# Grouped and differential attention of a layer as one stage over one list of items

## The chip, the cores and the metric

The kernel runs on one core of one Trainium2 chip. The core has a matrix engine (TensorE, PE in the rows; PEld is its weight load), a vector engine (VectorE, DVE), an activation engine (ScalarE, ACT), GpSimd (POOL) and SyncE (SP), which issues the DMAs. The time is the device time of one execution in microseconds. The median of three runs before the change is 3674.05 us (3666.71 to 3675.09).

## What is computed

The program is two models one behind the other on 512 tokens of width 1024, in float32. The second has two layers, and each layer holds two attentions over the same tokens. Everything else (projections, a state-space scan, a gated merge, a mixture of experts) is as it was. The two attentions of one layer, cut to what matters:

```python
def gqa_block_attention(q, k, v):          # 4 query heads of 64, 2 key heads
    scale = d ** -0.5
    ...
        logits = jnp.einsum('bqgrd,bkgd->bgrqk', qi, k).astype(jnp.float32) * scale
        probs = jax.nn.softmax(logits, axis=-1).astype(v.dtype)
        return jnp.einsum('bgrqk,bkgd->bqgrd', probs, v)
...
def diff_block_attention(q1, q2, k1, k2, v, lam, rel_bias):   # 4 heads, queries of 32
    ...
        p1 = jax.nn.softmax(jnp.einsum('bqhd,bkhd->bhqk', q1i, k1).astype(jnp.float32) * scale + bias, axis=-1)
        p2 = jax.nn.softmax(jnp.einsum('bqhd,bkhd->bhqk', q2i, k2).astype(jnp.float32) * scale + bias, axis=-1)
        w = (p1 - lam * p2).astype(v.dtype)
        return jnp.einsum('bhqk,bkhd->bqhd', w, v)
...
    for i in range(DEPTH):
        ...
        o_a = gqa_block_attention(q, k, a_v.reshape(b, s, A_KV_HEADS, A_HEAD_DIM))
        ...
        o_c = (rms_norm(o_c, g_diff[i]) * (1.0 - lam_init)).reshape(b, s, DIFF_HEADS * DIFF_V_DIM)
        ...
        branches = jnp.stack([o_a, o_b, o_c, o_d], axis=2)
```

## The kernel before

The program is a chain of stages. A stage (`stage`, L231) is one block of instruction streams, one stream for each engine, with its own semaphores. At its end all engines meet (L239 in the rows is the branch behind that meeting), so no instruction of the next stage starts before the slowest engine is through. Inside a stage each engine runs its stream in the written order and waits on semaphores. In each layer the stages are the projections (`mix_project`), the scan (`ssm_scan`), `grouped`, `differential`, `merge`, `out_stage`, then the mixture of experts.

`grouped` and `differential` both build a list of items and hand it to the same three routines, one for each engine. An item is two score maps of 128 queries against 512 keys, held in two PSUM banks (banks 0 and 1 for even items, 2 and 3 for odd ones). The steps of an item n, by the names that the texts use:

- **score(n)**, TensorE, L1027: two products, one for each map. Grouped items have 64 rows, differential ones 32.
- **shift(n)**, VectorE: the negative row maximum. A grouped item takes one reduction over both maps (L1096) and a tiny product (L1097), and its scores stay in PSUM. A differential item takes two custom instructions with their read-outs (L1102), which add the bias table and write the sums to SBUF.
- **exps(n)**, ScalarE: two exponentials with row sums (L1072 grouped, reading PSUM; L1075 differential, in SBUF in place).
- **weigh(n)**, VectorE: the reciprocal (L1110) and the division, two instructions for a grouped item (L2034), three for a differential one (L2184 to L2186), whose two maps become one.
- **turn(n)**, TensorE, L1036: transposes into banks 6 and 7, eight for a grouped item (two maps), four for a differential one.
- **copy(n)**, ScalarE, L1083: the transposed maps from PSUM to SBUF, 1024 or 512 columns.
- **values(n)**, TensorE, L1044: products with the values, sixteen matrix instructions for a grouped item, eight for a differential one, into bank 4 (first half of the items) or bank 5 (second half).

TensorE's stream is score(0), score(1), and then for each n: score(n+2), turn(n), values(n-1), and values of the last item at the end. ScalarE's is exps(0), and for each n exps(n+1), copy(n). VectorE's is shift(0), and for each n shift(n+1), weigh(n). There are three score buffers in SBUF (`SB`) and two for the transposed maps (`PT`).

`grouped` has 8 items. Banks 4 and 5 hold its result; when the values of all 8 are summed, ScalarE copies both banks to SBUF (L2056) and the stage ends. At its start SyncE issues the load of the bias table (L2044, 1792 KB), into memory that the scan used until then, and waits for it. `differential` has 16 items, again into banks 4 and 5, and a norm over each head: ScalarE squares and copies a bank (L2218, L2219) behind item 9 and at the end, TensorE sums and spreads (L2200, L2210), VectorE multiplies (L2239).

## Time and profile before

| | us |
|---|---|
| median of three runs (lowest, highest) | 3674.05 (3666.71, 3675.09) |
| profiled execution, its device time | 3673.06 |
| its span, first to last instruction | 3671.3 |
| TensorE busy | 3474.4 (95% of the span) |
| VectorE busy | 1718.2 (47%) |
| ScalarE busy | 1147.7 (31%) |
| mean granted TensorE clock | 0.969 of full speed |

TensorE's busy time is no measure of its pace, because its instructions overlap and their ends are modelled; a start time is read instead. PEclk is the clock that TensorE was granted, as a share of 2.4 GHz: 1.00 is 2.4 GHz, 0.50 is 1.2 GHz, and a value between is a stretch with both. In a timeline row the bracket tells how long the engine was idle before the row and what released it.

### The profile page before, as it was taken

Reading aid. Unit: us, or ns where it says so; the run is one execution under the profiler, and the core shown is the slowest. Engines: PE = TensorE matmul, PEld = TensorE weight load, DVE = VectorE, ACT = ScalarE, POOL = GpSimd, SP = SyncE. Lnnn points to the kernel's source line nnn. Section 1 sums busy time; section 2 is a strip of 40 time slices with the busy share of each in tenths; the row PEclk is TensorE's granted clock in tenths of the full one; section 3 lists DMA queues with packets and bytes.
Section 4 is the critical chain, followed back from the end, with each engine's and each line's share of the span. In section 5 each row is a group of like instructions: output and inputs, shape, how many; then the busy total and the mean of one; then the engine's idle time right before and its main releaser. Section 6 shows DMA issues by size and latency. Waiting matters only on the chain. (4 is left out here: it accounts for less than half of the span.)

```text
span 3671.3 us, 44737 instructions
## 1 busy us (share of the span) xinstructions
PE 3474.4 (95%) x16808; PEld 2376.3 (65%) x16808; DVE 1718.2 (47%) x2898; ACT 1147.7 (31%) x1816; POOL 41.5 (1%) x20
## 2 busy tenths in 40 slices
PE   8899999989999999989998999999988997999997
PEld 6678877855788886746875444437756886444436
DVE  6665545468665537566334111137656334111116
ACT  6632223147422224365322000013355333000003
POOL 0000000022000000000000000000000000000000
PEclk9999999999999999989999999999988998999998
DMA  4223322210133231211225999991211324999992
GB/s 153 89 91 94 96 91 97 81 71 1 69 97 96 92 97 55 70 61 55 98 95 203 405 421 422 422 381 58 90 61 34 98 80 173 376 421 422 422 421 82
DMA packets 113080, 618.90 MB, mean 169 GB/s; under 512 B 12780, under 2 KB 13300, under 8 KB 63544
## 3 DMA queue, kind: packets, MB, share of 16 engines
q1 hardware_dynamic: 112952, 617.18, 44.1%
q8 instruction: 82, 1.34, 0.1%
q14 instruction: 46, 0.38, 0.0%
HBM read 614.95 MB, written 4.28 MB: 169 GB/s over the span
## 5 line engine op out<-in xcount | busy, mean ns | idle before, releaser
L400 PE MATMUL PS<-WK_r,RING_r 128*128 128x512 f32 x1920 | 748.7, 390 | 0.0
L398 PE MATMUL PS<-WK_r 128*128 128x512 f32 x1448 | 565.1, 390 | 0.8 <-DVE RING_r L395 0.8
L400 PEld LDWEIGHTS PS<-WK_r,RING_r 128*128 128x128 f32 x1920 | 360.0, 187 | 77.2
L392 ACT ACTIVATE WK_r<-RING 128x1024 fp32r<-128x1024 f32 x212 | 223.4, 1054 | 449.7 <-PE PS L400 369.9
L399 PE MATMUL PS<-HT_r,WK_r 128*128 128x512 f32 (+1 forms) x896 | 348.6, 389 | 0.0
L395 DVE TENSOR_TENSOR RING_r<-RING,WK_r 128x1024 fp32r<-128x1024 f32 x212 | 259.0, 1221 | 184.9 <-ACT WK_r L392 184.8
L398 PEld LDWEIGHTS PS<-WK_r 128*128 128x128 f32 x1448 | 271.3, 187 | 58.4 <-DVE RING_r L395 1.3
L399 PE MATMUL PS<-HT_r,RING_r 128*128 128x512 f32 (+1 forms) x752 | 296.4, 394 | 0.0
L400 PE MATMUL PS<-AR_r,RING_r 128*128 128x512 f32 x672 | 262.9, 391 | 0.0
L395 DVE TENSOR_TENSOR RING_r<-RING,RING_r 128x1280 fp32r<-128x1280 f32 (+2 forms) x96 | 132.3, 1380 | 275.3 <-ACT RING_r L392 275.3
L398 PE MATMUL PS<-AR_r,RING_r 128*128 128x512 f32 x640 | 251.2, 392 | 9.1 <-DVE HT_r L395 9.1
L399 PE MATMUL PS<-AR_r,WK_r 128*128 128x512 f32 (+1 forms) x552 | 214.7, 389 | 0.0
L392 ACT ACTIVATE RING_r<-RING 128x1280 fp32r<-128x1280 f32 (+2 forms) x96 | 113.6, 1185 | 288.3 <-PE PS L400 263.2
L2644 DVE TENSOR_TENSOR XT<-XT,PS 128x512 f32<-128x512 f32 x128 | 82.1, 684 | 235.9 <-PE PS L2540 235.9
L399 PEld LDWEIGHTS PS<-HT_r,WK_r 128*128 128x128 f32 (+1 forms) x896 | 167.7, 187 | 35.8 <-issue 0.5
L2524 PE MATMUL PS<-AR,WK 128*64 128x512 f32 x768 | 171.6, 595 | 0.0
L395 DVE TENSOR_TENSOR AR_r<-AR,WK_r 128x512 fp32r<-128x512 f32 (+1 forms) x74 | 51.2, 692 | 239.8 <-ACT WK_r L392 239.6
L399 PEld LDWEIGHTS PS<-HT_r,RING_r 128*128 128x128 f32 (+1 forms) x752 | 141.8, 189 | 32.3 <-issue 1.3
L2658 DVE TENSOR_TENSOR HT<-HT,PS 128x512 f32<-128x512 f32 x32 | 20.6, 684 | 301.6 <-PE PS L2510 301.6
L2491 PEld LDWEIGHTS PS<-WK 128*128 128x128 f32 x896 | 107.4, 191 | 68.2 <-issue 68.2
L400 PEld LDWEIGHTS PS<-AR_r,RING_r 128*128 128x128 f32 x672 | 127.3, 189 | 26.5
L398 PEld LDWEIGHTS PS<-AR_r,RING_r 128*128 128x128 f32 x640 | 121.2, 189 | 35.3 <-DVE RING_r L395 9.9
(458 smaller groups left out, 5357.5 us busy)
## 6 DMA issues: line engine op xcount, KB each, us to landing
AR<-moe SPq DMA_DIRECT2D x192, 1024.0 KB, 16.4
RING<-moe SPq DMA_DIRECT2D x160, 1024.0 KB, 15.9
RING<-ff_in SPq DMA_DIRECT2D x96, 512.0 KB, 3.5
RING<-branch SPq DMA_DIRECT2D x64, 640.0 KB, 3.8
WK<-moe SPq DMA_DIRECT2D x32, 1024.0 KB, 17.7
RING<-ff_out SPq DMA_DIRECT2D x48, 512.0 KB, 3.5
RING<-mix_in SPq DMA_DIRECT2D x44, 512.0 KB, 3.5
RING<-ple SPq DMA_DIRECT2D x16, 640.0 KB, 9.1
```

The costliest lines, as they stand in the source:

```text
L392: return nc.scalar.activation(r(out), x, ACT.Copy)
L395: return nc.vector.tensor_tensor(r(out), x, r(high).bitcast(F32), ALU.subtract)
L398: nc.tensor.matmul(out, r(w_high), r(x_high), start=start, stop=False)
L399: nc.tensor.matmul(out, r(w_high), r(x_low), start=False, stop=False)
L400: return nc.tensor.matmul(out, r(w_low), r(x_high), start=False, stop=stop)
L2491: mm = nc.tensor.matmul(bank(k // 4, (k % 4) * P, P), HN[:, t, k * P:(k + 1) * P], HOTS[parity][:, t], start=(t == 0), stop=(t == TT - 1))
L2524: mm = nc.tensor.matmul(bank(4 + half)[e * CAP:(e + 1) * CAP], HI[:, k, e * CAP:(e + 1) * CAP], w[:, (2 * row + e) * TOK:(2 * row + e + 1) ...
L2644: v.tensor_tensor(XT[:, k], XT[:, k], bank(k - 4 if spread else 6 + k % 2), ALU.add).then_inc(s["added"], 1)
L2658: v.tensor_tensor(HID[:, half], SG[:, half], bank(2 + half), ALU.mult).then_inc(s["hidden"], 1)
```

## The change

`grouped` and `differential` become one stage, `attention`, with one list of 24 items: the 8 grouped ones (0 to 7) and behind them the 16 differential ones (8 to 23, `FIRST` is 8). The three routines take a list of both kinds: how many signals an item of either kind gives is counted from the list (`shifted`, and the sum over `values`), where it was a fixed multiple. The grouped results leave their banks while later items run: ScalarE copies bank 4 behind copy(5) and bank 5 behind copy(9) (`output`), and TensorE waits for that copy before the first values of item 8 (bank 4) and of item 16 (bank 5) (`bank_free`). The load of the bias table keeps its place at the stage's start, and VectorE waits for it before shift(8).

```diff
@@ -1014,24 +1014,26 @@
             self.scores, self.bias, self.weigh, self.values, self.outs = scores, bias, weigh, values, outs
             self.scale = scale
 
-    def att_pe(pe, s, items, then=lambda n: None):
-        maps = len(items[0].values)
-
+    def shifted(items, n):
+
+        return sum(1 if x.bias is None else 2 for x in items[0:n + 1])
+
+    def att_pe(pe, s, items, then=lambda n: None, before=lambda n: None):
         def score(n):
             if n >= 2:
-                if items[n].bias is None:
+                if items[n - 2].bias is None:
                     pe.wait_ge(s["exped"], 2 * (n - 1))
                 else:
-                    pe.wait_ge(s["maxed"], 2 * (n - 1))
+                    pe.wait_ge(s["maxed"], shifted(items, n - 2))
             for m, (q, k) in enumerate(items[n].scores):
                 mm = nc.tensor.matmul(bank(2 * (n % 2) + m), q, k, start=True, stop=True)
             mm.then_inc(s["scored"], 1)
 
         def turn(n):
-            pe.wait_ge(s["weighed"], maps * (n + 1))
+            pe.wait_ge(s["weighed"], sum(len(x.values) for x in items[0:n + 1]))
             if n:
                 pe.wait_ge(s["copied"], n)
-            for m in range(maps):
+            for m in range(len(items[n].values)):
                 for kb in range(TT):
                     mm = nc.tensor.transpose(bank(6 + m, kb * P, P), SB[n % 3][:, m, kb * P:(kb + 1) * P], cst("ident"))
             mm.then_inc(s["turned"], 1)
@@ -1039,6 +1041,7 @@
         def values(n):
             x = items[n]
             pe.wait_ge(s["copied"], n + 1)
+            before(n)
             for kb in range(TT):
                 for m, out in enumerate(x.outs):
                     mm = nc.tensor.matmul(out, x.values[m][kb], PT[n % 2][:, m, kb * P:kb * P + P],
@@ -1057,15 +1060,13 @@
         values(len(items) - 1)
 
     def att_act(act, s, items, then=lambda n: None):
-        maps = len(items[0].values)
-
         def exps(n):
             if items[n].bias is None:
-                act.wait_ge(s["maxed"], n + 1)
+                act.wait_ge(s["maxed"], shifted(items, n))
                 if n >= 3:
                     act.wait_ge(s["turned"], n - 2)
             else:
-                act.wait_ge(s["maxed"], 2 * (n + 1))
+                act.wait_ge(s["maxed"], shifted(items, n))
             for m in range(2):
                 buf = SB[n % 3][:, m]
                 if items[n].bias is None:
@@ -1080,6 +1081,7 @@
             act.wait_ge(s["turned"], n + 1)
             if n >= 2:
                 act.wait_ge(s["summed_v"], n - 1)
+            maps = len(items[n].values)
             nc.scalar.activation(PT[n % 2][:, 0:maps], PS[:, 6:6 + maps], ACT.Copy).then_inc(s["copied"], 1)
 
         exps(0)
@@ -1098,6 +1100,8 @@
                 return
             if n >= 3:
                 dve.wait_ge(s["turned"], n - 2)
+            if items[n - 1].bias is None:
+                dve.wait_ge(s["bias"], 16)
             for m in range(2):
                 nc.vector.tensor_tensor_reduce(SB[n % 3][:, m], bank(2 * (n % 2) + m), items[n].bias, 1.0, 3e38,
                                                ALU.add, ALU.min, NM[n % 3][:, m:m + 1]).then_inc(s["maxed"], 1)
@@ -2025,40 +2029,16 @@
                     evict(f"ck{c}", ar(CK + c))
 
 
-    def grouped(l):
-        with stage("bias o_out" + ATT) as (block, s):
-            items = []
-            for c in range(2):
-                for t in range(TT):
-                    def weigh(step, p, rc, co):
-                        return [nc.vector.tensor_scalar(p[:, m], p[:, m], rc[:, m:m + 1], None, ALU.mult)
-                                for m in range(2)]
-
-                    halves = [slice(0, 64), slice(64, 128)]
-                    items.append(Item([(ar(AQ + c)[rows, t * P:(t + 1) * P], ar(AK)[rows]) for rows in halves], None, weigh,
-                                      [[VM[:, kb, q * 64:q * 64 + 64] for kb in range(TT)] for q in range(2)],
-                                      [bank(4 + c, t * P, P)[rows] for rows in halves], RQ[:, t, 2 * c:2 * c + 2]))
-
-            @block.sync
-            def _(sp):
-                sp.dma_start(BIAS, skewed).then_inc(s["bias"], 16)
-                sp.wait_ge(s["bias"], 16)
-
-            @block.tensor
-            def _(pe):
-                att_pe(pe, s, items)
-
-            @block.scalar
-            def _(act):
-                att_act(act, s, items)
-                act.wait_ge(s["summed_v"], len(items))
-                for c in range(2):
-                    nc.scalar.activation(wk(BR + c), bank(4 + c), ACT.Copy).then_inc(s["o_out"], 1)
-
-            @block.vector
-            def _(dve):
-                step = Steps(dve, s["dve_step"])
-                att_dve(dve, s, step, items)
+    def grouped_items():
+
+        def weigh(step, p, rc, co):
+            return [nc.vector.tensor_scalar(p[:, m], p[:, m], rc[:, m:m + 1], None, ALU.mult) for m in range(2)]
+
+        halves = [slice(0, 64), slice(64, 128)]
+        return [Item([(ar(AQ + c)[rows, t * P:(t + 1) * P], ar(AK)[rows]) for rows in halves], None, weigh,
+                     [[VM[:, kb, q * 64:q * 64 + 64] for kb in range(TT)] for q in range(2)],
+                     [bank(4 + c, t * P, P)[rows] for rows in halves], RQ[:, t, 2 * c:2 * c + 2])
+                for c in range(2) for t in range(TT)]
 
 
     def ssm_scan(l):
@@ -2169,11 +2149,18 @@
 
 
     BIAS = ar(7, 7).rearrange("p (h m) -> p h m", h=4)
-    def differential(l):
+    def attention(l):
         RH = SM[:, 312:312 + 4 * TT].rearrange("p (t c h) -> p t c h", t=TT, c=2)
         lam_init = 0.8 - 0.6 * float(np.exp(-0.3 * l))
-        with stage("o_done" + ATT + HEAD_NORM) as (block, s):
-            items = []
+        with stage("bias o_out o_done" + ATT + HEAD_NORM) as (block, s):
+            items = grouped_items()
+            FIRST = len(items)
+
+            @block.sync
+            def _(sp):
+                sp.dma_start(BIAS, skewed).then_inc(s["bias"], 16)
+                sp.wait_ge(s["bias"], 16)
+
             for c in range(2):
                 for hh in range(2):
                     h = 2 * c + hh
@@ -2201,7 +2188,11 @@
                                               start=True, stop=True)
                     mm.then_inc(s["hn_summed"], 1)
 
-                att_pe(pe, s, items, lambda n: head_sums(0) if n == 10 else None)
+                def bank_free(n):
+                    if n in (FIRST, FIRST + 8):
+                        pe.wait_ge(s["o_out"], 1 + (n - FIRST) // 8)
+
+                att_pe(pe, s, items, lambda n: head_sums(0) if n == FIRST + 10 else None, bank_free)
                 head_sums(1)
                 pe.wait_ge(s["hn_inverse"], 1)
                 for c in range(2):
@@ -2214,11 +2205,21 @@
             @block.scalar
             def _(act):
                 def square(c):
-                    act.wait_ge(s["summed_v"], 8 * (c + 1))
+                    act.wait_ge(s["summed_v"], FIRST + 8 * (c + 1))
                     nc.scalar.activation(wk(10 + c), bank(4 + c), ACT.Square).then_inc(s["hn_squared"], 1)
                     nc.scalar.activation(wk(BR + 4 + c), bank(4 + c), ACT.Copy, scale=par("diff_g", l)).then_inc(s["hn_copied"], 1)
 
-                att_act(act, s, items, lambda n: square(0) if n == 9 else None)
+                def output(c):
+                    act.wait_ge(s["summed_v"], TT * (c + 1))
+                    nc.scalar.activation(wk(BR + c), bank(4 + c), ACT.Copy).then_inc(s["o_out"], 1)
+
+                def between(n):
+                    if n in (TT + 1, 2 * TT + 1):
+                        output(n // TT - 1)
+                    if n == FIRST + 9:
+                        square(0)
+
+                att_act(act, s, items, between)
                 square(1)
                 act.wait_ge(s["hn_mean"], 1)
                 nc.scalar.activation(RH, RH, ACT.Sqrt).then_inc(s["hn_root"], 1)
@@ -2758,8 +2759,7 @@
     for l in range(LAYERS):
         mix_project(l)
         ssm_scan(l)
-        grouped(l)
-        differential(l)
+        attention(l)
         merge(l)
         out_stage(mix_out[l], arc, load_router(l), None if l else (lambda k: nc.vector.scalar_tensor_tensor(
             out=XT[:, k], in0=XT[:, k], scalar=par("final1_g", k), in1=R1, op0=ALU.mult, op1=ALU.mult)))
```

ScalarE, around the end of the grouped items in layer 0. Before (L1072 and L1075 are the exponentials, L1083 the copies of transposed maps, L2056 the copies of the grouped result):

```order
L1072 ACTIVATE WK,SM<-PS,SM 128x512 x2
L1083 ACTIVATE WK<-PS 128x1024
L1072 ACTIVATE WK,SM<-PS,SM 128x512 x2
L1083 ACTIVATE WK<-PS 128x1024 x2
L2056 ACTIVATE WK<-PS 128x512 x2
L239 UNCONDITIONAL_BRANCH
L2214 UNCONDITIONAL_BRANCH
L1075 ACTIVATE WK,SM<-WK,SM 128x512 x4
L1083 ACTIVATE WK<-PS 128x512
```

After, with L1073 and L1076 for the exponentials, L1085 for the copies of maps and L2214 for the copy of one result bank:

```order
L1085 ACTIVATE WK<-PS 128x1024
L2214 ACTIVATE WK<-PS 128x512
L1073 ACTIVATE WK,SM<-PS,SM 128x512 x2
L1085 ACTIVATE WK<-PS 128x1024
L1076 ACTIVATE WK,SM<-WK,SM 128x512 x2
L1085 ACTIVATE WK<-PS 128x1024
L1076 ACTIVATE WK,SM<-WK,SM 128x512 x2
L1085 ACTIVATE WK<-PS 128x512
L1076 ACTIVATE WK,SM<-WK,SM 128x512 x2
L1085 ACTIVATE WK<-PS 128x512
L2214 ACTIVATE WK<-PS 128x512
```

The two result copies stood together in front of the branch; now each stands alone between a copy of maps and the next exponentials, four items apart.

TensorE, the same place in layer 0. Before (L1036 transposes, L1044 values, L1027 scores), from the transposes of item 6:

```order
L1036 MATMUL PS<-CST,WK 128x128 x8
L1044 MATMUL PS<-WK,AR 64x128 x8
L1036 MATMUL PS<-CST,WK 128x128 x8
L1044 MATMUL PS<-WK,AR 64x128 x16
L239 UNCONDITIONAL_BRANCH
L2195 UNCONDITIONAL_BRANCH
L1027 MATMUL PS<-AR 128x512 x6
L1036 MATMUL PS<-CST,WK 128x128 x4
L1027 MATMUL PS<-AR 128x512 x2
L1036 MATMUL PS<-CST,WK 128x128 x4
L1044 MATMUL PS<-WK,AR 64x128 x4
```

After, with L1029 for the scores, L1038 for the transposes and L1047 for the values, from the scores of item 8:

```order
L1029 MATMUL PS<-AR 128x512 x2
L1038 MATMUL PS<-CST,WK 128x128 x8
L1047 MATMUL PS<-WK,AR 64x128 x8
L1029 MATMUL PS<-AR 128x512 x2
L1038 MATMUL PS<-CST,WK 128x128 x8
L1047 MATMUL PS<-WK,AR 64x128 x8
L1029 MATMUL PS<-AR 128x512 x2
L1038 MATMUL PS<-CST,WK 128x128 x4
L1047 MATMUL PS<-WK,AR 64x128 x8
L1029 MATMUL PS<-AR 128x512 x2
L1038 MATMUL PS<-CST,WK 128x128 x4
L1047 MATMUL PS<-WK,AR 64x128 x4
```

The branch is gone, and the scores of items 8 and 9 stand in front of the transposes of items 6 and 7. VectorE, the same place, before (L1110 reciprocal, L2034 division, L1102 bias and maximum):

```order
L1096 TENSOR_REDUCE SM<-PS 128x2
L1097 TENSOR_TENSOR SM<-SM 128x2
L1110 RECIPROCAL SM<-SM 128x2
L2034 TENSOR_SCALAR WK<-WK,SM 128x512 x2
L1110 RECIPROCAL SM<-SM 128x2
L2034 TENSOR_SCALAR WK<-WK,SM 128x512 x2
L239 UNCONDITIONAL_BRANCH
L2226 UNCONDITIONAL_BRANCH
L1102 ISA WK,SM<-PS,AR 128x512
L1102 ISA SM 128x1
```

After (L1114 reciprocal, L2035 division, L1106 bias and maximum), from the division of item 6:

```order
L2035 TENSOR_SCALAR WK<-WK,SM 128x512 x2
L1106 ISA WK,SM<-PS,AR 128x512
L1106 ISA SM 128x1
L1106 ISA WK,SM<-PS,AR 128x512
L1106 ISA SM 128x1
L1114 RECIPROCAL SM<-SM 128x2
L2035 TENSOR_SCALAR WK<-WK,SM 128x512 x2
L1106 ISA WK,SM<-PS,AR 128x512
L1106 ISA SM 128x1
L1106 ISA WK,SM<-PS,AR 128x512
L1106 ISA SM 128x1
L1114 RECIPROCAL SM<-SM 128x2
```

The shifts of items 8 and 9 now stand in front of the weighing of items 7 and 8.

## Rows read from the trace of the kernel before

**Rows 1.** Busy time by stretch: both attention stages together, layer 0 and layer 1

```profile
core 0: us, PE busy (x) PEld busy (x) DVE busy (x) ACT busy (x) POOL busy (x), PEclk, DMA share, GB/s
...
1598.04:1691.24 93.20, 81.90 (x528) 49.66 (x528) 64.73 (x172) 59.39 (x129) 0.00 (x0) 0.87 0.06 21
...
2716.70:2811.93 95.23, 84.50 (x528) 51.36 (x528) 64.91 (x172) 59.36 (x129) 0.00 (x0) 0.84 0.06 21
```

**Rows 2.** Timeline, grouped items in layer 0, at their steady pace

```profile
1618.76 1.09 PE L1036 MATMUL PS<-CST,WK 128*128 128x128 f32 x8
...
1619.89 1.02 ACT L1083 ACTIVATE WK<-PS 128x1024 f32<-128x1024 f32 x1 [0.56 <-PE PS L1036]
...
1620.81 1.13 PE L1027 MATMUL PS<-AR 64*128 64x512 f32 x4
...
1621.87 1.09 PE L1036 MATMUL PS<-CST,WK 128*128 128x128 f32 x8
```

**Rows 3.** Timeline, from the last grouped item to the first differential one, layer 0

```profile
1627.75 2.28 PE L1044 MATMUL PS<-WK,AR 128*64 128x128 f32 x32
...
1630.07 1.08 ACT L2056 ACTIVATE WK<-PS 128x512 f32<-128x512 f32 x2 [1.20 <-PE PS L1044]
...
1631.46 1.99 PE L1027 MATMUL PS<-AR 32*128 32x512 f32 x8 [1.44 <-PEq L239]
...
1637.26 1.12 PE L1036 MATMUL PS<-CST,WK 128*128 128x128 f32 x4 [1.19 <-DVE WK L2186]
```

**Rows 4.** Timeline, TensorE's transposes and VectorE of differential items 3 to 12, layer 0

```profile
1644.69 0.69 DVE L1102 CUSTOM_DVE_ANT_0 WK<-PS,AR 128x512 f32<-128x512 f32 x1 [1.36 <-PE PS L1027]
...
1647.63 0.66 PE L1036 MATMUL PS<-CST,WK 128*128 128x128 f32 x4 [0.33 <-DVE WK L2186]
...
1650.43 0.66 PE L1036 MATMUL PS<-CST,WK 128*128 128x128 f32 x4
...
1670.52 0.66 PE L1036 MATMUL PS<-CST,WK 128*128 128x128 f32 x4 [0.19 <-DVE WK L2186]
...
1674.17 0.66 PE L1036 MATMUL PS<-CST,WK 128*128 128x128 f32 x4
```

**Rows 5.** Timeline, transposes around the same seam in layer 1

```profile
2739.57 1.09 PE L1036 MATMUL PS<-CST,WK 128*128 128x128 f32 x8
...
2755.43 1.12 PE L1036 MATMUL PS<-CST,WK 128*128 128x128 f32 x4 [1.21 <-DVE WK L2186]
...
2758.48 1.11 PE L1036 MATMUL PS<-CST,WK 128*128 128x128 f32 x4
...
2763.43 1.12 PE L1036 MATMUL PS<-CST,WK 128*128 128x128 f32 x4
...
2770.68 0.66 PE L1036 MATMUL PS<-CST,WK 128*128 128x128 f32 x4 [0.33 <-DVE WK L2186]
```

**Rows 6.** Busy time by stretch (columns as Rows 1), around the seam, layers 0 and 1

```profile
1622.00:1631.00 9.00, 7.29 (x88) 5.85 (x88) 3.38 (x8) 5.95 (x11) 0.00 (x0) 1.00 0.00 0
...
1634.00:1640.00 6.00, 4.81 (x12) 1.72 (x12) 5.42 (x16) 4.49 (x12) 0.00 (x0) 0.50 0.00 0
...
1646.00:1655.00 9.00, 8.41 (x53) 4.73 (x50) 8.58 (x27) 6.61 (x16) 0.00 (x0) 1.00 0.00 0
...
2760.00:2765.00 5.00, 5.00 (x18) 2.84 (x18) 2.82 (x9) 2.05 (x6) 0.00 (x0) 0.50 0.01 3
```

**Rows 7.** Issue and landing of the bias table in layer 0

```profile
AR<-bias_spread SPq DMA_DIRECT2D x1, 1792.0 KB, 7.6
```

**Rows 8.** Timeline of SyncE: first DMAs behind the attention, both layers

```profile
1691.24 0.81 SPq L259 DMA_DIRECT2D RING<-mix_out  x2
...
1965.61 2.48 SPq L2365 DMA_DIRECT2D RING<-moe  x5
...
2811.93 0.81 SPq L259 DMA_DIRECT2D RING<-mix_out  x2
...
3086.29 2.45 SPq L2365 DMA_DIRECT2D RING<-moe  x5
```

## Prediction

> **What bounds the kernel now.** The first view is the busy time by stretch. The two attention stages together take 93.20 us in layer 0 and 95.23 us in layer 1 [rows 1], 188.4 us of a span of 3671.3 us, so the change can touch one twentieth of the program. The reader should see there that no engine fills this stretch (TensorE 81.90, VectorE 64.73, ScalarE 59.39 of 93.20 us) and that the same instructions take 2.03 us longer in layer 1 at a lower clock (0.84 against 0.87).
>
> The second view is the timeline, to see who waits at the steady pace. A grouped item takes 3.11 us (transposes at 1618.76 and 1621.87) and TensorE shows no idle time ahead of its rows, while ScalarE waits 0.56 us in each item [rows 2]. TensorE bounds the grouped items. A differential item takes 2.86 us: from 1647.63 to 1670.52 there are eight of them [rows 4], and there TensorE waits 0.33 and 0.19 us for VectorE. VectorE bounds these: from the start of its shift at 1644.69 to the transposes that follow its weighing at 1647.63 are 2.94 us [rows 4].
>
> The third view is the seam between the stages. TensorE's last grouped values begin at 1627.75, ScalarE then copies the result for 1.08 us, all engines meet, the first differential scores start at 1631.46 after 1.44 us of idle time, and the first differential transposes come at 1637.26 [rows 3]. The clock was 1.00 until 1631, is 0.50 from 1634 to 1640 and 1.00 again from 1646 on; in layer 1 it is still 0.50 at 2760 to 2765 [rows 6]. So the seam costs three things: a pipeline that runs empty and fills again, the meeting itself, and a stretch at 1.2 GHz instead of 2.4 GHz.
>
> **The change, part by part.** I price it as one interval, from the transposes of grouped item 5 to those of differential item 4, which is item 12 of the merged list. Ahead of it nothing in TensorE's stream changes, behind it both kernels are at the steady pace.
>
> Before, layer 0: 1650.43 - 1621.87 = 28.56 us [rows 2, 4]. Before, layer 1: 2770.68 - 2739.57 = 31.11 us [rows 5].
>
> After, the interval holds seven items' steps. The scores of item 8 go where scores always stand, one item's pace behind those of item 7: 1620.81 + 3.10 = 1623.91 [rows 2]. The waits of item 8 have been met by then: the exponentials of item 6 that free its banks run ahead of those scores, and the bias table, issued at the start of the stage, lands after 7.6 us [rows 7] and is needed only some 27 us in. The three steps of TensorE's loop follow each other at 1.06, 1.02 and 1.02 us (scores at 1620.81 to transposes at 1621.87 is the first [rows 2]; the other two share the rest of 3.11), so the transposes of items 6, 7 and 8 come at 1624.97, 1628.07 and 1631.17, still bound by TensorE. VectorE keeps up: the scores of item 9 start at 1627.01 and take 1.13 us [rows 2], so its shift starts at about 1628.25 and item 8 is weighed 2.94 us later, at 1631.19. The scores of item 10 start at 1630.11 and end at 1631.24; its shift starts at 1631.35, and the transposes of item 9 follow at 1634.29. From here VectorE is the bound at 2.86 us: item 12 at 1634.29 + 3 x 2.86 = 1642.87. That makes 21.0 us for the interval. For layer 1 I take the same 21.0 us, since the clock is as high there ahead of the seam.
>
> - Layer 0: 28.56 - 21.0 = 7.6 us gone. Layer 1: 31.11 - 21.0 = 10.1 us gone. Together 17.7 us.
>
> The added work is ScalarE's result copies, two in each layer. They are not new, they only move, 0.54 us each [rows 3]. Behind copy(5) the copy of bank 4 falls into the 0.56 us in which ScalarE waits in each grouped item [rows 2]. In numbers: copy(4) ends at 1619.89 + 1.02 = 1620.91, copy(5) one pace later at 1624.02, the result copy at 1624.56, and the two exponentials of item 7, which fill what is left of an item (3.11 - 0.56 - 1.02 = 1.53 us), at 1626.09. VectorE wants them only behind the shift of item 8, whose two instructions of 0.69 us [rows 4] start at 1625.15 and are through at 1626.5. Behind copy(9) ScalarE has more room still. So I take nothing for them. If that cover is gone, the nearest row is the place where the kernel already squares and copies a bank inside the list, behind differential item 9: the transposes stand 3.65 us apart there (1670.52 to 1674.17 [rows 4]), 0.8 us over the pace, with sums of the head norm on TensorE in it as well. That bounds an insertion at 0.8 us, 3.2 us for four. From below, no item can be faster than 2.86 us; if all seven were, the interval would be 20.0 us, a further 2.0 us for both layers.
>
> The two waits of TensorE for the freed banks (ahead of the first values of items 8 and 16) have the values queued behind them, and VectorE waits for nobody there; the copies they wait for end about 10 us (bank 4) and 20 us (bank 5) earlier. VectorE's wait for the bias table has the shift of item 8 behind it and is long met. These cost nothing.
>
> What lies behind the attention moves as a whole. SyncE issues nothing of it inside the attention; the first load of the experts comes 274.37 us after the merge's first load in layer 0 and 274.36 us in layer 1 [rows 8]. So neither transfers nor clock behind the attention depend on how long it took, and the gain is not given back there.
>
> The sum against the profiled execution's own time: 3673.06 - 17.7 = 3655.4 us. The profiled execution lies 1.0 us under the median of the three runs, 3674.05, which is inside their spread of 8.4 us. With the bounds of the copies and of the pace this case reaches from 3653.4 to 3658.6 us.
>
> **The rivals.**
>
> Rival 1: the clock falls near the old seam all the same. For it speaks that it falls at 1634, where TensorE has been idle for no more than 1.44 us at a time [rows 3, 6]. Against it: in the merged list TensorE has the scores of items 8 and 9 to do where it now waits. Its price is the part of the present gain that the clock makes: from the first to the fifth differential transposes are 13.17 us in layer 0 (1637.26 to 1650.43 [rows 3, 4]) and 15.25 us in layer 1 [rows 5] where four items at the pace take 11.44 us; 1.7 + 3.8 = 5.5 us. That gives 3655.4 + 5.5 = 3660.9 us.
>
> Rival 2, the slower one: the clock stays low for much of the merged list. The differential items leave TensorE a small gap in each item [rows 4], and two TensorE groups of different kinds now alternate. An item fully at 1.2 GHz takes 4.95 us (2758.48 to 2763.43 [rows 5]), 2.09 us over the pace. The gain is used up from 17.7 / 2.09 = 8.5 such items in the two lists of 16; if half of them, 16, ran so, the loss would be 33.4 us and the time 3655.4 + 33.4 = 3688.8 us. Against it: with the same gaps the clock is 1.00 from 1646 on [rows 6]. The Trainium skill says in "TensorE: Matmul & The Clock Gate", section "A second HAM failure mode: psum-queue depth-cycling", that a kernel which cycles through PSUM banks and idles briefly between groups of matmuls lets its clock swing between the two levels and loses throughput to it; by that rule this would be the outcome. By that rule, the trace disagrees so far.
>
> Rival 3: the lists interlock badly where they meet. Scores wait on another signal for a differential item than for a grouped one, and if one of the engines meets an empty queue once, a whole item's latency shows. The price is that of a first item's chain, 5.80 us from first scores to first transposes (1631.46 to 1637.26 [rows 3]) less the 2.86 us it would have taken: 2.9 us in each layer, 3661.3 us. The step by step reckoning above speaks against it; it rests on start times of before.
>
> Rival 4: the gain is hidden or given back, because the experts' loads or another later stage set the end whatever comes first; 3673 us. The rows of SyncE speak against it [rows 8].
>
> **How the numbers follow.** The forecast has 0.70, rival 1 has 0.13, rival 2 has 0.03, rival 3 has 0.09, rival 4 has 0.05. The predicted time is 3655.4 us. For the range, the low end is the forecast's own, 3653.4, less half the spread of the runs, 4.2: 3649 us. The high end takes in rivals 1 and 3 with some of that spread: 3664 us. A measurement of this kernel can tell about 0.3%, 11 us, from no change, so faster means under 3663.0 us. The forecast lies there nearly whole (0.67), rivals 1 and 3 lie just under the bound (0.12 of their 0.22). That makes faster 0.79, same 0.18 with rival 4 and the rest, slower 0.03.
>
> **What would show it.** In the changed profile the attention of layer 0 should take 85.6 us and of layer 1 85.1 us, nearly alike, with a mean clock above 0.9 in both. The transposes of items 5 and 12 should stand 21.0 us apart in both. The clock should be 0.50 only at the stage's start and not again before the head norm. Between the transposes of items 8 and 9 there should be about 3.1 us, afterwards 2.86 us. ScalarE's two result copies should have TensorE and VectorE unmoved behind them. The merge's first load should come 7.6 us earlier than now, and the last instruction 17.7 us earlier. I am wrong if the clock is 0.50 in the middle of the list, if an item around the meeting of the two kinds takes over 4 us, or if the stretches behind the attention have grown.

## The result, and the profile after

The changed kernel took 3653.20 us, the median of 5 runs (3647.95 to 3656.47), beside 3666.71 us for the kernel before in the same comparison, also 5 runs. The ratio is 0.9949 (0.9936 to 0.9962). Two more comparisons of the same pair, on two different chips, gave 0.9955 (0.9942 to 0.9969) and 0.9960 (0.9947 to 0.9974). Over all comparisons the median is 3670.52 us for the kernel before (75 runs, 3661.51 to 3681.38) and 3654.58 us for the changed one (15 runs, 3647.95 to 3658.81). The ratios are not the quotients of two medians (of the first comparison that would be 0.9963), so the gain is best given as a span: 15.9 us by the medians over all comparisons, 18.7, 16.5 and 14.7 us (of 3670) by the three ratios, 13.5 us by the medians of the first comparison. That is 0.4 to 0.5%. I had forecast 17.7 us and 3655.4 us.

The busy time by stretch of the changed kernel, for the attention of both layers, and for the merged list of each layer without its first items and its head norm. Columns as in [rows 1]:

```profile
core 0: us, PE busy (x) PEld busy (x) DVE busy (x) ACT busy (x) POOL busy (x), PEclk, DMA share, GB/s
1596.33:1680.24 83.91, 75.97 (x528) 46.73 (x528) 64.66 (x172) 59.16 (x129) 0.00 (x0) 0.95 0.07 23
2707.45:2792.05 84.60, 76.95 (x528) 46.79 (x528) 64.65 (x172) 59.27 (x129) 0.00 (x0) 0.93 0.07 23
...
1606.00:1677.00 71.00, 65.86 (x479) 41.31 (x479) 57.12 (x158) 53.41 (x119) 0.00 (x0) 1.00 0.01 1
...
2721.00:2790.00 69.00, 63.86 (x466) 40.13 (x468) 54.95 (x154) 51.14 (x114) 0.00 (x0) 1.00 0.00 1
```

Against [rows 1] the attention is 9.29 us shorter in layer 0 and 10.63 us in layer 1, with the same 528 records of matrix instructions. VectorE and ScalarE do the same work in the same time (64.66 and 59.16 us). TensorE is busy 5.93 us less in layer 0, though no product is gone: the products that ran at a clock of 0.50 now run at 1.00. Where [rows 6] had 0.50 (1634 to 1640), the clock is now 1.00, and so it is from 1606 to 1677.

The timeline of the changed kernel, layer 0, answers to [rows 2 to 4]. It goes from the transposes of item 5 to those of item 12, which are those of differential item 4 (L1038 transposes, L2214 copy of a result bank, L1106 bias and maximum, L2173 the last instruction of a weighing):

```profile
1618.91 1.09 PE L1038 MATMUL PS<-CST,WK 128*128 128x128 f32 x8
...
1620.95 0.59 ACT L2214 ACTIVATE WK<-PS 128x512 f32<-128x512 f32 x1
...
1622.01 1.09 PE L1038 MATMUL PS<-CST,WK 128*128 128x128 f32 x8
1622.13 0.69 DVE L1106 CUSTOM_DVE_ANT_0 WK<-PS,AR 128x512 f32<-128x512 f32 x1 [0.69 <-PE PS L1029]
...
1625.12 1.10 PE L1038 MATMUL PS<-CST,WK 128*128 128x128 f32 x8
...
1628.22 0.66 PE L1038 MATMUL PS<-CST,WK 128*128 128x128 f32 x4
...
1631.29 0.66 PE L1038 MATMUL PS<-CST,WK 128*128 128x128 f32 x4 [0.32 <-DVE WK L2173]
...
1632.47 0.59 ACT L2214 ACTIVATE WK<-PS 128x512 f32<-128x512 f32 x1
...
1634.09 0.66 PE L1038 MATMUL PS<-CST,WK 128*128 128x128 f32 x4
...
1637.01 0.66 PE L1038 MATMUL PS<-CST,WK 128*128 128x128 f32 x4 [0.20 <-DVE WK L2173]
...
1639.81 0.66 PE L1038 MATMUL PS<-CST,WK 128*128 128x128 f32 x4
```

The interval is 1639.81 - 1618.91 = 20.90 us; the sum said 21.0. In layer 1 it is 20.92 us (2731.24 to 2752.16). Items 5 to 8 stand 3.10, 3.11 and 3.10 us apart, where TensorE is the bound; then 3.07 us, and from there 2.80, 2.92 and 2.80 us, where VectorE is. VectorE shifts the first differential item at 1622.13, in the middle of grouped items, and TensorE's longest idle time where the kinds meet is the 0.32 us at 1631.29.

The rest of the attention's difference between the two profiles lies at its two ends. With the interval's 7.66 and 10.19 us taken off, 1.6 us remain in layer 0 and 0.4 us in layer 1. The start (first scores to the transposes of item 5) took 22.58 and 23.79 us in place of 23.83 and 22.87, the end (item 12 to the merge) 40.43 and 39.89 in place of 40.81 and 41.25. The instructions there are unchanged, and the experiments below show the same times wander between executions of one kernel.

### The profile page after: what moved, and what is told of

Read it like the earlier page. It is cut to its first block and busy times, and to the rows that moved or that the text cites. A ratio compares the mean times of both kernels' runs of the same rounds, so it can differ in the third digit from the quotient of the medians.

```text
span 3650.2 us, 44715 instructions
## 1 busy us (share of the span) xinstructions
PE 3460.2 (95%) x16808; PEld 2369.7 (65%) x16808; DVE 1718.2 (47%) x2898; ACT 1147.3 (31%) x1816; POOL 41.6 (1%) x20
## 6 DMA issues: line engine op xcount, KB each, us to landing
RING<-moe SPq DMA_DIRECT2D x160, 1024.0 KB, 16.5
```

## The experiments

Fillers below are products of two identity matrices into a bank that the next real product overwrites; nobody reads what they write. They are there to keep TensorE at work. Intervals are always those from the transposes of item 5 to those of item 12 (of differential item 4, in the kernel before), layer 0 and then layer 1.

**The kernel before, once more.** No edit. The question was whether its runs fall into two levels and whether the single profiled execution was a fair sample.

> The kernel before, unchanged, for a second profile and more times. Its runs so far lie at two levels, about 3666.3 us (three) and 3674.5 us (two). Theory A: the levels are clock phases (how long TensorE stays at 1.2 GHz behind a seam), so the upper level has the lower mean clock and a profile of the lower level shows the two attention stretches shorter than 93.20 and 95.23 us, down to about 92 each. Theory B: the levels come from elsewhere (transfers of the experts); then the attention stretches are again 93.2 and 95.2 us and the difference lies in the experts' stretches.

It took 3671.88 us (11 runs, 3662.5 to 3680.42), ratio 1.0 (0.9989 to 1.0011). The runs spread evenly over 18 us, so the runs show no two levels. The intervals were 28.55 and 31.12 us, within 0.01 us of the first profile. What did differ is shown by the first scores of the attention, the first row in the profile before and the second in this one:

```profile
1598.09 3.79 PE L1027 MATMUL PS<-AR 64*128 64x512 f32 x8 [1.76 <-PEq L239]
```

```profile
1602.75 3.79 PE L1027 MATMUL PS<-AR 64*128 64x512 f32 x8 [1.76 <-PEq L239]
```

The same instructions ahead of the attention took 4.7 us longer this time. And in layer 1 the start took 21.36 us, not 22.87, so that this layer's attention was 93.48 us against 95.23. The interval that the change acts on is sharp; what lies around it is not.

**The changed kernel, once more and a third time.** No edit.

> The changed kernel, unchanged, for a second profile and more times. Attention 83.9 and 84.6 us as in its first profile, within 1 us, if the clock holds at 1.00 from the grouped items to the head norm each time; up to 5 us more in one layer if the clock sometimes falls at the old seam. Time 3648 to 3656 us.

The changed kernel took 3656.35 us (5 runs, 3651.32 to 3658.81), ratio 0.9955. Intervals 20.91 and 20.91 us; attention 83.34 and 85.25 us.

> The changed kernel, unchanged, beside the one with filler. If its gain is 17.7 us in the long run, it takes 16 to 19 us less than the kernel before of the same session, interval 20.9 us in both layers. If the 13.5 us of the first comparison is the true size, 12 to 15 us less.

The third time it took 3654.99 us (5 runs, 3652.8 to 3657.45), ratio 0.9960. Intervals 20.91 and 20.91 us; attention 83.80 and 85.17 us. The interval repeats to 0.02 us in three profiles and six layers, while layer 1's attention moved by 0.65 us. The medians of the three comparisons differ by 13.5, 14.7 and 12.8 us, under the 17.7 us of the sum each time; but a ratio of 1 - 17.7 / 3670 = 0.9952 lies inside each of the three intervals. The last comparison (12.8 us by the medians, 14.2 by the means) falls into the band of 12 to 15 us that had been written down for the smaller gain, not into 16 to 19.

**The list emptied at the old seam.** The changed kernel, but all engines finish item 7 before item 8 enters. This puts back the empty pipeline alone: no meeting of the engines, and the result copies stay off the path.

```diff
+    DRAIN = 8
...
         for n in range(len(items)):
-            if n + 2 < len(items):
+            if n + 2 < len(items) and n not in (DRAIN - 2, DRAIN - 1):
                 score(n + 2)
             turn(n)
-            if n:
+            if n and n != DRAIN:
                 values(n - 1)
                 then(n - 1)
+            if n == DRAIN - 1:
+                values(n)
+                score(n + 1)
+                score(n + 2)
...
```

ScalarE's exponentials and VectorE's shift of item 8 go behind item 7 in the same way.

> The merged stage, but the list runs empty at the old seam: the scores of items 8 and 9 come behind the values of item 7, and the exponentials and the shift of item 8 behind the copy and the weighing of item 7. No meeting of the engines, no result copies on the path. If the gain is the pipeline that no longer runs empty (with the clock that goes with it), the interval from the transposes of item 5 to those of item 12 goes from 20.9 us back to 25 to 27 us in each layer and most of the gain is lost (time about 3661 to 3664 us). If the gain is the meeting of the engines and the result copies, the interval stays within 1.5 us of 20.9 us and the time within 3 us of the changed kernel's.

This kernel took 3667.99 us (11 runs), ratio 0.9991 (0.9981 to 1.0). Intervals 29.29 and 27.27 us, more than the 25 to 27 that had been expected. Nearly all of the gain is gone, so the meeting and the copies were not the main part of what the seam cost. The timeline of TensorE at the drained place, layer 0, and the clock there:

```profile
1638.34 1.13 PE L1031 MATMUL PS<-AR 32*128 32x512 f32 x4 [0.55 <-DVE SM L1114]
1641.59 0.66 PE L1040 MATMUL PS<-CST,WK 128*128 128x128 f32 x4 [2.13 <-DVE WK L2183]
1642.18 1.97 PE L1031 MATMUL PS<-AR 32*128 32x512 f32 x4
```

```profile
core 0: us, PE busy (x) PEld busy (x) DVE busy (x) ACT busy (x) POOL busy (x), PEclk, DMA share, GB/s
1638.00:1642.00 4.00, 1.53 (x8) 0.71 (x8) 3.53 (x11) 2.93 (x8) 0.00 (x0) 1.00 0.02 4
1642.00:1646.00 4.00, 3.76 (x14) 1.70 (x13) 3.82 (x15) 2.47 (x6) 0.00 (x0) 0.54 0.00 0
1646.00:1650.00 4.00, 4.00 (x14) 2.17 (x13) 1.64 (x3) 2.03 (x6) 0.00 (x0) 0.50 0.00 0
```

TensorE waits 0.55 us and 2.13 us for VectorE's chain on the first differential item, and behind this the clock falls: the two scores of one item (L1031, four records) take 1.13 us at 1638.34 and 1.97 us at 1642.18. In both layers of this run the empty pipeline brings the low clock with it. To price the two apart the clock must be held.

**The drained list, clock held.** As above, with 8 fillers in the waits of the first differential item.

```diff
+            if n == DRAIN:
+                fill(6, 7)
             turn(n)
...
+            if n == DRAIN - 1:
+                values(n)
+                score(n + 1)
+                score(n + 2)
+                fill(6, 1)
```

> The drained list once more (scores of item 8 behind the values of item 7), with 8 products of a constant in TensorE's idle time at the seam, 1 behind the scores of item 9 and 7 ahead of the transposes of item 8, to hold the clock. If emptying and clock are two separate parts of the loss, the clock stays at 1.00 and the interval from the transposes of item 5 to those of item 12 is 14.4 + 11.4 = about 25.8 us in both layers, against 29.3 and 27.3 us drained without filler and 20.9 us in the changed kernel: 5 us a layer for the emptying alone. If the clock does not follow TensorE's activity here, the interval stays at 27 to 29 us.

This kernel took 3663.05 us (11 runs), ratio 0.9984 (0.9974 to 0.9993). The intervals were 25.69 and 25.68 us, alike in both layers, and 25.8 had been expected. The same two views, with the transposes of items 5 and 12 at the timeline's ends:

```profile
1626.90 1.09 PE L1044 MATMUL PS<-CST,WK 128*128 128x128 f32 x8
...
1637.38 0.49 PE L1021 MATMUL PS<-CST 128*128 128x128 f32 x2
1638.00 1.13 PE L1035 MATMUL PS<-AR 32*128 32x512 f32 x4
1639.06 1.83 PE L1021 MATMUL PS<-CST 128*128 128x128 f32 x14
1641.26 0.66 PE L1044 MATMUL PS<-CST,WK 128*128 128x128 f32 x4 [0.38 <-DVE WK L2190]
1641.85 1.13 PE L1035 MATMUL PS<-AR 32*128 32x512 f32 x4
...
1652.59 0.66 PE L1044 MATMUL PS<-CST,WK 128*128 128x128 f32 x4
```

```profile
core 0: us, PE busy (x) PEld busy (x) DVE busy (x) ACT busy (x) POOL busy (x), PEclk, DMA share, GB/s
1642.00:1646.00 4.00, 2.91 (x18) 1.72 (x20) 3.82 (x13) 3.23 (x8) 0.00 (x0) 1.00 0.00 0
1646.00:1650.00 4.00, 3.74 (x22) 1.78 (x19) 3.82 (x11) 3.36 (x9) 0.00 (x0) 1.00 0.00 0
```

L1021 are the fillers (each counts as two). They end before VectorE has weighed the item (0.38 us of idle time is left ahead of the transposes), so they delay nothing, and the clock stays at 1.00. An empty pipeline at full clock costs 25.69 - 20.91 = 4.8 us in each layer.

**The kernel before, clock held.** Fillers at the seam of the kernel before, 24 of them: 12 behind the last grouped values, 4 and 8 around the first differential item.

```diff
         score(1)
+        if items[0].bias is not None:
+            fill(6, 4)
         for n in range(len(items)):
             if n + 2 < len(items):
                 score(n + 2)
+            if n == 0 and items[0].bias is not None:
+                fill(6, 8)
             turn(n)
...
                 att_pe(pe, s, items)
+                fill(6, 12)
```

> The kernel before, with idle time of TensorE at the seam filled with 24 products of a constant (128 by 128) whose results nobody reads: 12 behind the last grouped values, 4 behind the first two differential scores, 8 ahead of the first differential transposes. If the half clock behind the seam comes from TensorE's idle time there, the clock stays at 1.00 or returns sooner, and the interval to differential item 4 shrinks from 28.6 and 31.1 us by 1.7 and 3.8 us to about 27 us in both layers (about 5.5 us of the program). If the clock falls for another reason, nothing shrinks, or it grows by up to 2 us a layer by the filler itself.

This kernel took 3669.10 us (11 runs), ratio 0.9992 (0.9983 to 1.0001). The clock was 1.00 across the seam in both layers, yet the intervals were 28.44 and 28.44 us. The timeline shows why:

```profile
1630.08 2.95 PE L1019 MATMUL PS<-CST 128*128 128x128 f32 x24
1633.32 1.99 PE L1031 MATMUL PS<-AR 32*128 32x512 f32 x8 [0.30 <-PEq L239]
1635.23 1.16 PE L1019 MATMUL PS<-CST 128*128 128x128 f32 x8
1636.32 1.13 PE L1031 MATMUL PS<-AR 32*128 32x512 f32 x4
1637.38 2.05 PE L1019 MATMUL PS<-CST 128*128 128x128 f32 x16
```

The first twelve take 2.95 us, longer than the wait they were to fill, and hold up the meeting and the first scores; the last eight are still running when the item has been weighed. From the transposes of item 7 to those of item 8 there are now 12.40 us in place of 10.51. It was too much filler: the clock is held, but the interval alone does not show what that is worth. With the 1.9 us of delay taken off it is 26.5 us in both layers, which is an estimate of the seam at full clock.

**The same with fewer fillers.** 10 instead of 24: 4 behind the last grouped values, 1 and 5 around the first differential item.

> The kernel before with 10 filler products in place of 24 (4 behind the last grouped values, 1 behind the first two differential scores, 5 ahead of the first differential transposes). With 24 the first differential scores came 1.9 us later because the filler outlasted ScalarE's result copies. If only that hid the gain, the interval to differential item 4 is now about 26.5 us in both layers (28.44 less 1.9), with the clock at 1.00: 2 and 4.6 us under the kernel before, some 6 us of the program. If the lesser filler does not hold the clock, it is 28 to 31 us as before.

This kernel took 3668.32 us (12 runs), ratio 0.9993 (0.9983 to 1.0004). It came out mixed, and that made it useful. In layer 0 the clock held and the interval was 26.71 us, as expected. In layer 1 the clock fell at the transposes of item 9 and the interval was 29.72 us, though the instructions are the same and the transposes of items 5 and 8 stand 15.38 us apart in both. The transposes of items 5, 9, 10 and 12, first in layer 0 and then in layer 1:

```profile
1615.59 1.09 PE L1040 MATMUL PS<-CST,WK 128*128 128x128 f32 x8
...
1633.77 0.66 PE L1040 MATMUL PS<-CST,WK 128*128 128x128 f32 x4 [1.08 <-DVE WK L2195]
...
1636.57 0.66 PE L1040 MATMUL PS<-CST,WK 128*128 128x128 f32 x4
...
1642.30 0.66 PE L1040 MATMUL PS<-CST,WK 128*128 128x128 f32 x4
...
2733.90 1.09 PE L1040 MATMUL PS<-CST,WK 128*128 128x128 f32 x8
...
2752.08 0.84 PE L1040 MATMUL PS<-CST,WK 128*128 128x128 f32 x4 [1.09 <-DVE WK L2195]
...
2756.76 1.11 PE L1040 MATMUL PS<-CST,WK 128*128 128x128 f32 x4
...
2763.62 0.66 PE L1040 MATMUL PS<-CST,WK 128*128 128x128 f32 x4 [0.32 <-DVE WK L2195]
```

So 26.71 us is the seam of the kernel before at full clock, and the 26.5 us of the run before it agrees to 0.2 us. The difference to the drained list, 26.71 - 25.69 = 1.0 us, I put down to the meeting of the engines with the two result copies. It is what is left over; no run takes it out alone.

**The result copies doubled.** The changed kernel, each copy of a result bank issued twice (the extra one to a place that is written later anyway).

```diff
                     act.wait_ge(s["summed_v"], TT * (c + 1))
+                    nc.scalar.activation(wk(BR + 4 + c), bank(4 + c), ACT.Copy)
                     nc.scalar.activation(wk(BR + c), bank(4 + c), ACT.Copy).then_inc(s["o_out"], 1)
```

> The changed kernel, but each bank of grouped results is copied twice by ScalarE in the list (first into a chunk that is free then, and then where it belongs): two more copies of 0.59 us a layer. If such a copy is hidden wholly, the interval from item 5 to item 12 stays at 20.9 us. If ScalarE's room in a grouped item (0.56 us) is all there is, the second copy behind item 5 shows with up to 0.6 us and the one behind item 9 with nothing, 21.5 us. If insertions cost 0.8 us each, it is 22.5 us.

This kernel took 3651.97 us (5 runs), ratio 0.9951 (0.9937 to 0.9965). Intervals 20.92 and 20.91 us, unchanged. ScalarE's timeline of this kernel at the first copy:

```profile
1620.57 1.02 ACT L1085 ACTIVATE WK<-PS 128x1024 f32<-128x1024 f32 x1 [0.56 <-PE PS L1038]
1621.48 0.59 ACT L2214 ACTIVATE WK<-PS 128x512 f32<-128x512 f32 x1
1621.96 0.60 ACT L2215 ACTIVATE WK<-PS 128x512 f32<-128x512 f32 x1
1622.44 0.79 ACT L1073 ACTIVATE WK<-PS,SM 128x512 f32<-128x512 f32 x1
...
1623.95 1.05 ACT L1085 ACTIVATE WK<-PS 128x1024 f32<-128x1024 f32 x1
```

The second copy of maps starts with no wait, where the first had 0.56 us: the two copies have eaten ScalarE's slack, and still nobody waits for it. So one copy costs nothing, as the sum had it, and there is room for a second.

**Clock held at the ends of the attention.** With the seam gone, the clock is low at the attention's start and in its head norm. The changed kernel with fillers at the end of the scan (7, 2, 5), around the first item (5, 1), in the head norm (2, 4, 3) and at the start of the merge (12).

```diff
         score(1)
+        fill(6, 5)
...
+            if n == 0:
+                fill(6, 1)
             turn(n)
...
+                fill(0, 7)
                 token_sums(pe, s, "squared", 2, [wk(10), wk(11)], 4)
+                fill(0, 2)
                 spread_tokens(pe, s, 5)
+                fill(0, 5)
...
```

> The changed kernel with filler products in the idle time of TensorE that is left around the attention: 7, 2 and 5 at the end of the scan stage, 5 and 1 behind the first scores of the attention, 2, 4 and 3 in the head norm, 12 ahead of the merge's first products. If the half clock at the attention's start and the merge's start comes from TensorE's idle time, the first five items take 1.5 to 2.5 us less in each layer and the merge's start 2 us less in each, 6 to 9 us of the program: about 3646 us where the changed kernel has 3654 us. If the fillers hold nothing, the time is the same or up to 3 us more.

This kernel took 3643.49 us (5 runs, 3641.17 to 3645.78), ratio 0.9925 (0.9911 to 0.9939). It beats both kernels. Attention by stretch, and TensorE at the end of the scan and the start of the attention in layer 0:

```profile
1598.94:1680.27 81.33, 76.37 (x558) 48.63 (x558) 64.57 (x172) 59.04 (x129) 0.00 (x0) 1.00 0.07 24
2704.88:2786.19 81.31, 76.37 (x558) 48.61 (x559) 64.58 (x172) 59.04 (x129) 0.00 (x0) 1.00 0.07 24
```

```profile
1589.91 1.83 PE L1019 MATMUL PS<-CST 128*128 128x128 f32 x14
1592.20 1.95 PE L317 MATMUL PS<-CST,WK 128*128 128x1 f32 x16 [0.47 <-ACT WK L2112]
...
1599.00 1.99 PE L1033 MATMUL PS<-AR 64*128 64x512 f32 x8 [0.30 <-PEq L239]
```

The changed kernel without fillers had this there:

```profile
1588.72 3.13 PE L317 MATMUL PS<-CST,WK 128*128 128x1 f32 x16 [2.23 <-ACT WK L2102]
...
1596.38 3.50 PE L1029 MATMUL PS<-AR 64*128 64x512 f32 x8 [1.76 <-PEq L239]
```

The eight records of the first scores take 1.99 us at full clock and 3.50 us without fillers. Attention is 81.3 us in both layers, now alike, against 83.9 and 84.6: 5.9 us together. From the start of the sums of L317 to the first scores it is 6.80 us against 7.66, 0.9 us more in each layer. That makes 7.6 us, and the spans of the two profiles differ by 7.4 (3650.2 and 3642.8). The medians differ by more, 11.1 us (3654.58 and 3643.49); no row here places the rest. Of what had been expected, the attention gained more (its start 2.2 and 3.4 us, not 1.5 to 2.5), and the merge, as the next run shows, nothing.

**The same without the merge's fillers.** Only the 12 at the start of the merge are left out.

> The kernel with filler around the attention, without the 12 products ahead of the merge. With them TensorE started the merge at 1.00 (0.50 without), yet the stretch from the merge's first load to the experts' first load was 273.95 and 273.83 us, inside the 273.8 to 274.95 us of the kernels without them. If the merge's start is bounded by ScalarE and VectorE, which prepare its operands, this kernel takes the same time with and without, within 2 us (3641 to 3646 us), with a merge stretch of 273.8 to 274.4 us again. If the filler did help, it is 3 to 4 us slower.

This kernel took 3644.08 us (5 runs, 3642.0 to 3646.8), ratio 0.9932 (0.9918 to 0.9945), which is 10.9 us under the changed kernel of the same comparison (3654.99). It has 273.96 to 274.58 us from the merge's first load to that of the experts, against 273.83 to 273.95. The fillers of the merge are worth nothing that can be told. As far as rows place it, the gain of the version above sits in the attention and right ahead of it.

## Why the prediction was right, and where it was off

**The interval.** Forecast 21.0 us in both layers, measured 20.90 and 20.92, and 20.91 in four more. That the scores of item 8 go where scores always stand, that TensorE bounds the items up to 8 and VectorE those behind, and the 3.1 us between items 8 and 9 (3.07) came out as worked. So did 28.56 and 31.11 for the kernel before, which its second profile gave again. The gain of this step, 7.6 + 10.1 us, is 7.66 + 10.19.

**What it consists of.** The runs split it into three parts:

| part | layer 0 | layer 1 | from |
|---|---|---|---|
| pipeline runs empty and fills | 4.8 | 4.8 | drained at full clock, 25.69, less 20.91 |
| engines meet, result copies | 1.0 | 1.0 | seam at full clock, 26.71, less 25.69 |
| half clock behind the seam | 1.9 | 4.4 | 28.56 and 31.11 less 26.71 |
| sum | 7.7 | 10.2 | |

The share of the clock had been priced at 1.7 + 3.8 = 5.5 us, as the price of rival 1. It measured 1.85 + 4.4 = 6.25 us. The price was small by 0.7 us because I took the low clock to begin to cost at the first differential transposes, and the pace of 11.44 us behind them. At full clock the four items take 11.33 us, and in layer 1 another 0.5 us lies ahead: items 5 to 8 took 31.11 - 15.25 = 15.86 us [rows 5], with the clock held 15.38. The 26.71 us has one layer of one profile behind it, beside the estimate of 26.5 us from the run with 24 fillers. The 1.0 us is the least certain of the three.

**The result copies and waits.** Forecast nothing, measured nothing: a second copy of each bank moves no interval by 0.02 us.

**What lies behind.** From the merge's first load to the experts' it is 274.95 and 273.96 us in the changed kernel, against 274.37 and 274.36 [rows 8]. The stretch moved as a whole, to 0.6 us, so rival 4 is out. The merge itself came 11.0 us earlier and not 7.6 (1680.24 against 1691.24 [rows 1]): 1.7 us of that lie ahead of the attention, and 1.6 at its two ends.

**Rivals 1 to 3.** The clock is 1.00 from 1606 to 1677 and from 2721 to 2790. The granted clock did not fall at the old seam (rival 1) and did not swing in the list (rival 2), though TensorE still shows gaps of 0.2 to 0.3 us in its differential items. The Trainium skill's "TensorE: Matmul & The Clock Gate", section "A second HAM failure mode: psum-queue depth-cycling", says that short idle times of this kind, in a kernel that cycles through PSUM banks, make the clock swing. The trace disagrees here: the granted clock was 1.00 over 71 us in layer 0 and over 69 us in layer 1, with such gaps in it. No item where the kinds meet took over 3.11 us (rival 3).

**The step that failed: the sum for the whole program.** The sum was 3673.06 - 17.7 = 3655.4 us, and it has two terms. The second is the interval's gain, and the profiles have that at 17.85 us. The step that failed is to take that gain for the gain of the whole program and to subtract it from one profiled execution, with everything outside the interval put at nothing. In the first comparison the kernel before took 3666.71 us, 6.4 us under the base, and the gain was 13.5 us where the sum has 17.7. The two errors cancel for the most part: 3655.4 us is 2.2 us from the measured 3653.20 and 0.8 us from the 3654.58 us of all comparisons, and that closeness is luck. With the right base of the first comparison the sum gives 3649.0 us, the very low end of the range.

Over all comparisons both errors are smaller. The kernel before has 3670.52 us, 2.5 us under the base and 3.5 us under the median of the three runs I had, whose spread should have told me that the base is not known better than that. From 3670.52 the sum gives 3652.8 us, 1.8 us less than the changed kernel takes. So the whole program's gain was too large by 1.8 us of 17.7 by all medians and by 4.2 us by the first comparison; the two profiled executions err to the other side, with 3673.06 - 3651.95 = 21.1 us. The chance of 0.79 for a faster kernel rests on a mark of 0.3%, for which the prediction shows no row. The gain passes that mark, but at 0.4 to 0.5% it is small, and against a mark of 2% it would be no change at all.

Is the shortfall real? The runs don't settle it. The ratios' intervals hold 17.7 us. The means of all runs (3670.62 and 3654.39 us) differ by 16.2 us, with two standard errors 14.5 to 18.0 us. The kernel with doubled copies, whose intervals are those of the changed kernel, has a ratio that makes 18.0 us. Three things are shown that could hold a real difference. The start of the attention wanders by more than 2 us (21.36 to 23.83 over two profiles of the kernel before, 22.56 to 23.79 over three of the changed one), and the program ahead of it by 4.7 us. The time of an execution goes with its mean granted clock: of 70 runs of the kernel before, the three at 0.967 took 3677.3 us on average and the five at 0.972 took 3664.1 us, so the base goes with how long TensorE is at half clock somewhere in the program; which causes which is not shown. And the loss behind a seam is itself not fixed: one edit that empties the list gave 29.29 us in one layer and 27.27 in the other. If layer 1 of the kernel before loses its 31.1 us in some executions only, the mean gain is under 17.7. I had two profiles of it, both with 31.1, and that is too few, so the cause stays open. The attention I forecast at 85.6 and 85.1 us was 83.9 and 84.6; the 1.7 us of layer 0 is such wandering at its ends, since its interval was met to 0.1 us.

## What to carry to other kernels

Price a seam between two stages as three things: the pipeline running empty and filling, the meeting, and the clock behind it; here they are 4.8 us, 1.0 us (by subtraction) and 1.9 to 4.4 us. Choose an interval from one steady place to another across the seam: it comes out of a timeline to 0.1 us and repeats to 0.02 us, while the whole program's time has a spread of 20 us (3661.51 to 3681.38) with no edit at all, so take the base from many runs and never from one profiled execution. Where a seam must stay, a few products that nobody reads can keep the clock up, and cost nothing if they end before the real work is ready; the fillers at the attention's ends were worth another 11 us by the medians (3654.99 to 3644.08 in one comparison), of which the rows place 7.6 us.

## What the runs showed of the hardware

The clock fell from 1.00 (2.4 GHz) to 0.50 (1.2 GHz) behind a place where TensorE's longest waits were 0.55 and 2.13 us, and eight fillers of 128x128, 2.3 us of TensorE's time (0.49 and 1.83), kept it at 1.00: 25.69 us in place of 29.29 and 27.27. Ten fillers in a row of spots at the old seam held it in one layer (26.71 us) and not in the other (29.72 us), with the same instructions at the same distances; where it fell, TensorE's longest wait from the first differential scores on had been 1.09 us. So the same code can be on either side, and one profile of a kernel near that edge is a sample, not the rule.

At half clock TensorE becomes the bound of items that VectorE bounds otherwise. In the drained list TensorE is busy for all of 1646 to 1650 and VectorE for 1.64 us of it; with the clock held they are busy for 3.74 and 3.82 us. The four items behind the seam took 14.94 us in place of 11.33.
